# Two activation buffers of a float32 two-block kernel begin 64 bytes later modulo 256

## The reference

```python
# block 1
z = rms_norm(h) @ w_in                       # 2048 x 5120: q, k, v, u, g
h = h + concat(diff_attention(q, k, v), gmlp_gate(gelu(u), gelu(g))) @ w_out
f = rms_norm(h)
h = h + (silu(f @ ffn_w1) * (f @ ffn_w3)) @ ffn_w2        # hidden 5632
h = h + (p @ pl_w_up) * sigmoid(h @ pl_w_gate)
x = rms_norm(h)
# block 2, with 16 meta tokens ahead of the 256
u, gb, gc, v, ga, gbr = split(rms_norm(h) @ w_in_2)       # 2048 x 12288
y_a = (pool(u) per group @ pool_w) * pool_scale
y_b = (gb * conv3(gc * v)) @ conv_out_w
h = h + (sigmoid(ga) * y_a + sigmoid(gbr) * y_b) @ w_o
h = h + (silu(hn @ w_gate) * (hn @ w_up)) @ w_down        # hidden 5632
out = rms_norm(h)[:, 16:]
```

## Time and profile before

| | us |
|---|---|
| median of three runs | 2670.3 |
| span of the profiled execution | 2668.2 |
| TensorE busy, matmul | 2657.2 |
| TensorE busy, weight load | 2349.5 |
| VectorE busy | 1658.2 |
| ScalarE busy | 1235.8 |
| GpSimd busy | 0.8 |

### The profile page before, as it was taken

The page is one execution under the profiler, slowest core; times in us unless marked ns, Lnnn a source line. Parts: engine busy times, 40 slices in busy tenths (PEclk is TensorE's granted clock), DMA queues, the critical chain, the costliest instruction groups (busy, mean ns, idle before and its releaser), DMA issues.

```text
span 2668.2 us, 39872 instructions
## 1 busy us (share of the span) xinstructions
PE 2657.2 (100%) x15711; PEld 2349.5 (88%) x15711; DVE 1658.2 (62%) x1645; ACT 1235.8 (46%) x1355; POOL 0.8 (0%) x7
## 2 busy tenths in 40 slices
PE   9999999999999999999999999999999999999998
PEld 7889888888888888888999999888888888888887
DVE  6567766555655556796676666556765645564555
ACT  5446554444444444565443333444554434443444
POOL 0000000000000000000000000000000000000000
PEclk9999999999999999999999999999999999999999
DMA  8554555556555555555555555555565555555554
GB/s 291 183 174 144 192 187 189 191 189 191 192 191 191 191 191 188 175 197 198 176 183 178 179 184 190 189 189 189 189 205 189 189 190 189 189 195 195 178 190 140
DMA packets 254251, 502.92 MB, mean 188 GB/s; under 512 B 8130, under 2 KB 11652, under 8 KB 253988
## 3 DMA queue, kind: packets, MB, share of 16 engines
q1 hardware_dynamic: 252180, 497.61, 56.5%
q10 hardware_dynamic: 1952, 3.68, 0.4%
HBM read 498.37 MB, written 2.88 MB: 188 GB/s over the span
## 4 chain that ended last, share of the span: by engine, by line
PE 99%; DVE 0%; ACT 0%; DMA 0%; issue 0%; ACTq 0%; DVEq 0%
PE ps L1356 49%; PE ps L1370 24%; PE ps L1389 4%; PE ps L1390 4%; PE ps L1391 4%; PE ps L1407 4%; PE ps L1408 4%; PE ps L1409 4%; PE ps L1399 0%; PE ps L1401 0%; PE ps L1400 0%; PE ps L1319 0%; DMA xtok<-in_x_dram 0%; PE ps L1543 0%; PE ps L1542 0%; PE ps L1544 0%
## 5 line engine op out<-in xcount | busy, mean ns | idle before, releaser
L822 DVE TENSOR_TENSOR lo<-raw,hi 128x1024 fp32r<-128x1024 f32 x940 | 1127.6, 1223 | 856.5 <-ACT hi L488 847.6
L488 ACT ACTIVATE hi<-raw 128x1024 fp32r<-128x1024 f32 x940 | 971.3, 1055 | 1065.3 <-PE ps L1370 479.0
L1356 PE MATMUL ps<-A,hi 128*128 128x512 f32 x3648 | 859.9, 392 | 0.0
L1356 PEld LDWEIGHTS ps<-A,hi 128*128 128x128 f32 x3648 | 675.1, 188 | 138.9
L1356 PE MATMUL ps<-B,hi 128*128 128x512 f32 x1984 | 481.7, 395 | 0.0
L1370 PEld LDWEIGHTS ps<-A,lo 128*128 128x128 f32 x3648 | 442.6, 188 | 11.5 <-DVE lo L822 0.2
L1370 PE MATMUL ps<-A,lo 128*128 128x256 f32 x3648 | 445.4, 278 | 0.0
L1356 PEld LDWEIGHTS ps<-B,hi 128*128 128x128 f32 x1984 | 364.4, 188 | 79.3
L1370 PEld LDWEIGHTS ps<-B,lo 128*128 128x128 f32 x1984 | 243.0, 188 | 10.3
L1370 PE MATMUL ps<-B,lo 128*128 128x256 f32 x1984 | 244.5, 277 | 0.0
L1408 PE MATMUL ps<-B,hi 128*128 128x258 f32 (+1 forms) x768 | 219.8, 286 | 0.0
(11 more groups left out here) (240 smaller groups left out, 1341.1 us busy)
## 6 DMA issues: line engine op xcount, KB each, us to landing
raw<-in_w_in_dram SPq DMA_DIRECT2D x136, 1024.0 KB, 5.1
raw<-in_ffn_w_dram SPq DMA_DIRECT2D x132, 1024.0 KB, 5.1
raw<-in_w_gate_up_dram SPq DMA_DIRECT2D x88, 1024.0 KB, 5.0
raw<-in_w_down_dram SPq DMA_DIRECT2D x44, 1024.0 KB, 5.1
raw<-in_w_out_dram SPq DMA_DIRECT2D x16, 1024.0 KB, 5.1
raw<-in_pl_w_gate_dram SPq DMA_DIRECT2D x16, 1024.0 KB, 5.1
raw<-in_conv_out_w_dram SPq DMA_DIRECT2D x16, 1024.0 KB, 5.1
raw<-in_w_o_dram SPq DMA_DIRECT2D x16, 1024.0 KB, 5.1
```

What stands on the lines that cost most here:

```text
L488: act.activation(hi[:, slot % RING], raw[:, raw_slot, 2 * (slot % 2):2 * (slot % 2) + 2, :], ACT.Copy).then_inc(hi_ready, 1)
L822: dve.tensor_tensor(lo[:, slot % RING], raw[:, slot // 2 % RAWS, 2 * (slot % 2):2 * (slot % 2) + 2, :], hi[:, slot % RING], ALU.subtract). ...
L1356: last = pe.matmul(ps[:, b0 + m, :], high(slot, kk, m), both, start=j == 0 and kk == 0, stop=ends and j == seg.pieces - 1 and kk == 1)
```

## The change

The declarations change places, and nothing else does. `r_row` goes in front of `A`; `vec1` (328 bytes), `ln_stats` (96) and `vec2` (384) go between `A` and `B`.

```diff
         rstd_meta = sb("rstd_meta", [P, META])
+        r_row = sb("r_row", [P, TM])
         A = sb("A", [P, KT, 2 * T], F32R)
-        r_row = sb("r_row", [P, TM])
+        vec1 = sb("vec1", [P, V1K])
+        ln_stats = sb("ln_stats", [P, 24])
+        vec2 = sb("vec2", [P, V2N])
@@
         ones = sb("ones", [P, P])
-        vec1 = sb("vec1", [P, V1K])
-        vec2 = sb("vec2", [P, V2N])
         small = sb("small", [P, 64])
@@
         tiny = sb("tiny", [P, 2, TM])
-        ln_stats = sb("ln_stats", [P, 24])
         metaT = sb("metaT", [P, KT, META])
```

## The result

The changed kernel takes 2694.2 us (median of four runs, 2694.05 to 2694.33) against 2670.25 before: 1.009 times as long, 95% interval 1.0078 to 1.0102. The profiled execution's span grew from 2668.2 to 2692.1 us, by 23.9.

A forecast was written before the change was run, and what follows sets the result against it. It took TensorE's matmul count times pitch as the bound; 7.3 - 1.0 - 4.7 - 0.9 + 0 + 4.3 + 8.7 = +13.7 us on 2668.2, plus 2.1 between span and median, gave 2684 us, range 2642 to 2712.

The forecast's parts named there:

- Bound and method: Whole kernel: time is the number of TensorE matmuls times their pitch, which the operands' distance modulo 256 decides.
- the meeting point: Stages on `B`, distance 0: both streams begin in the same place modulo 256, so the dearest pitch seen was taken.
- The prediction's own sign of being wrong: `A` `highs` runs below 7.33 us, `B` runs leaving 7.46, or 272- and 258-column pitches moving over a step.
- `A` `highs` at 128: 512-column matmuls streaming `A`: middle of 229.1 and 233.1 ns, +2.0 ons each over 3648, +7.3 us.
- all at the dearest seen: Upper bound, each width at its dearest pitch seen: +34 us together, of which `A` `highs` at 233.1 ns +14.6.
- `A` `lows` at 128: 256-column matmuls streaming `A`: middle of the 116 and 113.4 ns seen at 64 and 192, -4.7 us.
- The row of the wide form: Wide matmuls on `B`, high part at 128: 126.6 ns for 272 columns, read as 128 being no great gain.
- `B` at 0: Stages on `B`: `highs` stay at 233.1 ns, 0; token form to 233.1, +4.3 us; `lows` to 117.8, +8.7 us.
- Wide and conv: Wide and conv matmuls on `B`: left at 0, with 10 us either way put in the range.
- The rival "faster": 128 puts streams farthest apart and `B` leaves 192, dear for 512 columns: -21 us, 2649 us; chance 0.31.
- "No change": Pitch follows the address in a way the shift doesn't touch, or gain and loss cancel: 2670 us; chance 0.23.

## Why the prediction was right, and where it wasn't

**Bound and method** held. Nothing but the pitch changed: counts, VectorE's 1223 ns, the idle times ahead of TensorE are the old ones. The reading that four rows agree on a distance, not on a buffer, is what the run with the rings moved has shown: 2670.1 us with the changed kernel's `A` and `B`. The forecast was 2684, the measured time is 2694.2, inside the range of 2642 to 2712.

**The direction** came out right by luck. The sum of +13.7 us had next to nothing on `A` (+7.3 - 1.0 - 4.7 - 0.9 = +0.7) and all the rest on `B` (+13.0), because distance 0 was to be the meeting point. Measured it is the other way round: `A` alone cost 24.5 us, and `B` alone gained 2.1. The prediction's own sign of being wrong came about as well: runs of `highs` on `B` left 7.46 us, for 7.28. What it said would then hold, that the distance decides by another rule than nearness, is what the runs show.

**The size** came out of terms of which several were wrong and partly cancelled:

- `A` `highs` at 128: I took the middle of 64 and 192, +7.3 us; it is the dear level, 233.4 ns, +15.4. The pitch was within 0.3 ns of the bound of "all at the dearest seen".
- `A` `lows` at 128: the middle again, -4.7 us; measured +9.5. The sign was wrong, and with 14.2 us this is the largest miss. 118.5 ns is above both levels seen in the rows for this width, and so outside both bounds. The row of the wide form, 13.3 ns over its columns at 128, had pointed this way (118.5 is 11.8 over), and I weighed it only for the reading that 128 is no great gain.
- `B` at 0: I took the dearest for all. For `lows` that was right in kind (+8.7 forecast, +11.1 measured, 119.6 ns, again above the dearest seen). For `highs` and the token form it was wrong: 512 columns are cheapest at 0 (-9.5 us where I had 0, and -2.2 where I had +4.3). Within a run it is 226.7 ns, below the mean pitch of every 512-column form of the kernel before.
- Wide and conv: 0 forecast, -1.7 and +1.6 measured.

Two slips changed nothing: the prediction's own counts give 13088 matmuls, or 15392 with wide and conv, where it says 13500, and its range has "about 8 us" beyond the bounds where the wide and conv forms alone were to have 10.

What failed was the picture of two streams that are worst at distance 0 and better the farther apart they are. One picture for both widths can't hold: at 0 the 512-column matmuls are best and the 256-column ones worst. The measured table, with the runs' numbers, is

| distance | 512 columns, ns | 256 columns, ns |
|---|---|---|
| 0 | 226.7 in a run, 228 with its ends | 120 |
| 64 | 229 (the token form once 233.3) | 113.3 or 117.8 |
| 128 | 233.3 | 118.5 |
| 192 | 233.3 | 113.3, in few runs 117.8 |
| 32, 96 | 233.5 | 117, 120 |

It holds where `hi` and `lo` share a residue. The rival "faster" was tied to `A` `highs` below 229 at 128, and they rose. Its other half, that `B` leaves the distance that is dear for 512 columns, came true, with 9.5 us. "No change" fell with the pitches.

The Trainium skill's 16-byte lines (SBUF — State Buffer, section Specifications (TRN2)) would have left the time as it was, as the prediction said; steps of 32 and 64 bytes, all multiples of 16, moved this kernel by up to 1.3%. The Trainium skill's gap of N/2.4 + 2.5 ns (TensorE: Matmul & The Clock Gate, section Back-to-back issue gap), which the page gives for an isolated matmul, is 216 for 512 columns; the best measured here, with a weight load to each matmul, is 226.7.

## What to carry to other kernels

In a kernel that TensorE bounds, read the pitch from starts, or from a long run in the chain, for each form of matmul, and set it beside both operands' addresses: here 2% of the pitch (229 or 233 ns) hung on 64 bytes, and declaring a row of 1088 bytes in front of `A` and no longer behind it cost 24 us. Nothing tried was clearly better than the kernel before: the two widths want different distances, and the lowest time is 0.1% below it. Where a float32 operand is streamed beside a weight load, try both operands' residues modulo 256 at whole multiples of 64, each buffer alone; here the effects of the two buffers nearly added up (22.4 and 23.9 us). Moving the weights' ring by as many bytes as the activations is the cheap test of whether an effect is one of distance.

## What the runs showed of the hardware that was not expected

- The pitch of these matmuls depends on the distance of the streamed operand from the weights, modulo 256: 226.7 to 233.5 ns for 512 columns, 113.3 to 120 for 256, at a granted clock of 0.999 over each execution. The order is another for each width. The place of the weights being loaded has a part in it (232.5 for 226.7 ns with `lo` at 128); why it is so, and by what rule, the runs don't show.
- At 32 and at 96, inside a 64-byte block, 512-column matmuls take 233.5 ns, as much as at the worst multiple of 64.
- At one distance there can be two steady pitches, 113.3 and 117.8 ns for 256 columns, and 228.9 and 233.3 for the token form on `B`. So a change to one buffer can move a stage that doesn't read it, by 4.6 us here (the token form on `B` with `A` at 96). Which pitch is kept goes with what ran before, as far as the runs tell.
